# Filter spectra of a Hyena layer worked out in pieces between the expert passes

## What is computed

```
def hyena_filters(n, f_w1, f_b1, f_freq, f_w2, f_b2, f_w3):
    z = concatenate([t, cos(bands * w), -sin(bands * w)])      # positions alone
    h = sin(freq * (z @ f_w1 + f_b1))
    h = sin(freq * (h @ f_w2 + f_b2))
    h = (h @ f_w3).reshape(n, 2, C_ORDER, C_WIDTH)             # forward and backward filters
    return h * exp(-t * deltas)

def bidir_long_conv(u, h_fwd, h_bwd, bias):
    k = concatenate([h_fwd[:1] + h_bwd[:1], h_fwd[1:], 0, h_bwd[:0:-1]])
    uf = rfft(u, n=2 * n); kf = rfft(k)                        # kf: the spectrum of the filter
    return irfft(uf * kf)[:n] + u * bias
```

```
def expert_block(args):
    xb, e = args
    a = silu(xb @ w1[e]) * (xb @ w3[e])
    return a @ w2[e]
```

## Time and profile before

| | us |
|---|---|
| runs (3) | 3553.43, 3557.12, 3560.2; median 3557.12 |
| profiled execution, its own time | 3554.69 |
| its span in the profile | 3553.0 |
| TensorE busy | 3077.8 (87%) |
| VectorE busy | 1046.0 (29%) |
| ScalarE busy | 746.7 (21%) |
| DMA queue of SyncE (q1) | 416.81 MB, 33.2% of 16 engines' span |

### The profile page before, as it was taken

One profiled execution on the slowest core, in us unless ns is written; L12 is line 12 of the kernel. 1 busy time (PEld: TensorE's weight loads), 2 busy tenths in 40 slices (PEclk: granted clock), 3 DMA queues, 4 the chain that ended last, 5 costly groups with the idle time before them and its releaser, 6 DMA issues. The chain is left out here.

```text
span 3553.0 us, 34681 instructions
## 1 busy us (share of the span) xinstructions
PE 3077.8 (87%) x13906; PEld 1838.1 (52%) x13906; DVE 1046.0 (29%) x2162; ACT 746.7 (21%) x1627; POOL 164.0 (5%) x265
## 2 busy tenths in 40 slices
PE   6999974888887688999898999899948774888998
PEld 3448633444444655675455664465523343464674
DVE  3440622000000201254210472333025674200242
ACT  2111720000000202342200581100002210212341
POOL 0000001011111000000000120011100001000000
PEclk9999995899989899999999999999969887999999
DMA  6663441999999111200012100122233323011200
GB/s 229 232 232 131 174 153 44 380 377 384 386 386 337 60 53 32 76 1 24 1 36 72 72 2 1 45 84 97 77 108 155 129 77 124 0 42 55 76 1 24
DMA packets 244208, 441.15 MB, mean 124 GB/s; under 512 B 31420, under 2 KB 111820, under 8 KB 240725
## 3 DMA queue, kind: packets, MB, share of 16 engines
q1 hardware_dynamic: 234278, 416.81, 33.2%
q0 software_dynamic: 9776, 22.18, 1.8%
HBM read 408.73 MB, written 37.81 MB: 126 GB/s over the span
## 5 line engine op out<-in xcount | busy, mean ns | idle before, releaser
L347 PE MATMUL hyena_in_main<-hT,weight_slots 128*128 128x256 f32 (+1 forms) x1024 | 330.5, 486 | 1.4 <-PEq L988 1.4
L347 PEld LDWEIGHTS hyena_in_main<-hT,weight_slots 128*128 128x128 f32 x1024 | 194.6, 190 | 137.1 <-issue 124.0
L2006 PE MATMUL moe_ph<-expert_weights,moe_x_T 128*64 128x256 f32 x2048 | 235.8, 384 | 1.4 <-ACT moe_x_T L2159 1.4
L347 PE MATMUL swa_in_main<-hT,weight_slots 128*128 128x512 f32 (+1 forms) x576 | 189.3, 489 | 6.5 <-DMA weight_slots<-b_w_in 5.2
L2006 PEld LDWEIGHTS moe_ph<-expert_weights,moe_x_T 128*64 128x64 f32 x2048 | 144.6, 138 | 91.0 <-issue 24.7
L347 PE MATMUL mla_down_main<-hT,weight_slots 128*128 128x512 f32 (+1 forms) x448 | 168.6, 539 | 19.5 <-DMA weight_slots<-a_w_in 19.5
L1407 PE MATMUL qkv_main<-hT,weight_slots 128*128 128x512 f32 (+1 forms) x384 | 167.8, 580 | 0.9 <-PEq L988 0.9
L1198 PE MATMUL post_y<-expert_weights,hT 128*128 128x512 f32 x384 | 165.1, 592 | 0.0
L2023 PE MATMUL moe_py<-expert_weights,moe_act_T 128*64 128x512 f32 x512 | 161.4, 789 | 0.5 <-ACT moe_act_T L2166 0.5
L347 PEld LDWEIGHTS swa_in_main<-hT,weight_slots 128*128 128x128 f32 x576 | 110.0, 191 | 86.3 <-issue 73.7
L1996 PE MATMUL moe_px<-const_identity,moe_x 64*128 64x64 f32 x512 | 71.1, 294 | 90.1 <-DMA moe_x<-scr_tokens,moe_index 90.1
(11 more groups left out here) (357 smaller groups left out, 4117.4 us busy)
## 6 DMA issues: line engine op xcount, KB each, us to landing
expert_weights<-w SPq DMA_DIRECT2D x96, 2048.0 KB, 15.0
first_w_out<-w_mod SPq DMA_DIRECT2D x12, 2048.0 KB
expert_weights<-w_mod SPq DMA_DIRECT2D x12, 2048.0 KB, 8.0
weight_slots<-w_in SPq DMA_DIRECT2D x16, 1024.0 KB
weight_slots<-c_w_in SPq DMA_DIRECT2D x16, 1024.0 KB
weight_slots<-a_w_in SPq DMA_DIRECT2D x14, 1024.0 KB
scr_spectra<-expert_weights SPq DMA_DIRECT2D x12, 1024.0 KB, 3.8
expert_weights<-scr_spectra SPq DMA_DIRECT2D x12, 1024.0 KB, 5.3
```

What stands on the lines that cost most here:

```text
L347: mm = pe.matmul(main[u][0:unit.rows, 0:unit.cols], lhsT, rhs, start=(c == 0), stop=(c == r.kc - 1))
L2006: mm = pe.matmul(bank[half * T:(half + 1) * T, 0:HF], x_T[:, c, :], w[:, c, half * HF:(half + 1) * HF], start=(c == 0), stop=(c == KD - 1))
```

## The change

`filter_hidden` and `filter_spectra` are gone. Their work is in a class `FilterWork`, called from the streams of TensorE, ScalarE and VectorE in `experts_stage`. Each pass has three slots: slot 3b behind `turn_act`, 3b + 1 behind `turn_x`, 3b + 2 behind `down`. The two hidden products are in slots 2 and 5, with their six VectorE steps in the same slots and the Sin in slots 4 and 7; the sums of the filter weights are in slot 3. From slot 9 on 72 pieces are dealt out in order: 24 of filter rows (two products each) and 48 transform products (two 128x128 tiles each for x, one for the context). By the formula below they fall on slots 9 to 93, so into passes 3 to 31: 25 in slots 3b, 19 in 3b + 1, 28 in 3b + 2. Three PSUM banks are used in turn instead of eight; only the even products are copied by ScalarE, and VectorE forms sum and difference with the odd one straight from PSUM, in steps of 512 columns. The 12 stores of 1024 KB, three small loads and the load of the second half of the decays are issued by ScalarE, the stores two slots after their last product.

The other inputs (17 loads) are issued by SyncE in the route stage behind its own, which then waits for them. SyncE waits at the end of the expert stage for all spectra to be stored, before it issues `tiles` and the weight groups ahead. The eight transform tables of the convolution are loaded at the start of `hyena_in` (`beside`). `combine` takes its tiles from the arena of the expert weights, and the norm before the route takes its scratch from the weight slots.

```diff
@@ class FilterWork
+    SLOTS = 3
+    HID0, SIN0, HID1, SIN1, SUMS, FIRST = 2, 4, 5, 7, 3, 9
...
+        for j, (_, _, seg) in enumerate(self.jobs):
+            nb = SEGS[seg][2]
+            for c in range(2 * nb):
+                self.add(("rows", j, c), freed_by, ["rows", "rows"], cost, 1)
+            for k in range(nb):
+                for kind in range(KINDS):
+                    self.add(("kind", (j, k), kind), freed_by, ["odd" if kind % 2 else "even"], cost, nb)
+        self.banks = Banks(3, freed_by)
+        room, total, spent = self.SLOTS * (E - 1) - self.FIRST, sum(cost), 0
+        self.slot_of, taken = {}, set()
+        for piece, c in zip(self.pieces, cost):
+            slot = max(self.FIRST + spent * room // total, max(taken, default=0) + 1)
+            self.slot_of[piece] = slot
...
+    def on_tensor(self, pe, slot):
+        def free(q):
+            if q >= 3:
+                n = self.banks.upto(q - 3)
+                by = self.banks.freed_by[q - 3]
+                if by == "rows":
+                    pe.wait_ge(self.s_rows, n)
+                elif by == "even":
+                    pe.wait_ge(self.s_even, n)
+                else:
+                    pe.wait_ge(self.s_K, 2 * n)
+            return self.bank_of(q)
...
+            pe.wait_ge(self.s_rows, self.rows_upto(j))
+            pe.wait_ge(self.s_lag, j + 1)
+            b = free(q)
+            for c in range(nb):
+                row = kind % 2 * nb + c
+                mm = pe.matmul(b, table[seg][:, row, k * P:(k + 1) * P], src[:, row, :], start=(c == 0), stop=(c == nb - 1))
...
+    def on_scalar(self, act, scalar, slot):
...
+            act.wait_ge(self.s_K, 4 * (t + 1))
+            act.dma_start(self.spectra[SPECTRA.index((order, half, seg, k))], self.K[t % 2])\
+                .then_inc(self.s_stored[t % 2], 16)
...
+            act.wait_ge(self.s_mm, self.first_bank[piece] + 1)
+            if n >= 2:
+                act.wait_ge(self.s_K, 2 * (n - 1))
+            scalar.activation(self.parts[n % 2], self.bank_of(self.first_bank[piece]), ACT.Copy).then_inc(self.s_even, 1)
...
@@ def experts_stage
+                filters.finish(sp)
                 for tile, src in tiles:
                     sp.dma_start(tile, src).then_inc(s_tiles, 16)
@@ TensorE
                     if b:
                         turn_act(b - 1)
+                    filters.on_tensor(pe, n_slots * b)
                     pe.wait_ge(Stage.w3_in[b % 2], (b // 2 + 1) * 16)
                     pe.wait_ge(s_act, b)
                     up_product(pe, ph3, x_T[b % 2], experts.W3[b % 2]).then_inc(s_h3, 1)
                     if b + 1 < E:
                         turn_x(b + 1)
+                    filters.on_tensor(pe, n_slots * b + 1)
                     if b:
                         down(b - 1)
+                    filters.on_tensor(pe, n_slots * b + 2)
@@ VectorE
                 for b in range(E):
+                    filters.on_vector(dve, nc.vector, n_slots * b)
                     dve.wait_ge(s_silu, b + 1)
...
                     nc.vector.tensor_tensor(act_rows[:], ph3[:, 0:HF], act1[:], ALU.mult).then_inc(s_act, 1)
+                    filters.on_vector(dve, nc.vector, n_slots * b + 1)
                     if b:
                         copy_y(b - 1)
+                    filters.on_vector(dve, nc.vector, n_slots * b + 2)
@@ def route
+                for tile, src in beside:
+                    sp.dma_start(tile, src).then_inc(s_beside, 16)
+                sp.wait_ge(s_beside, 16 * len(beside))
@@ def hyena (was hyena_in and hyena_mix)
-    with nc.sbuf_tensor("filter_h2", [P, TOK], F32) as h2:
-        filter_hidden(nc, a, h2, tables)
-        filter_spectra(nc, a, h2, tables, spectra, g0, hT, left, consts)
-
+    hyena_in(nc, a, hT, scr, taps, consts,
+             [(tile, rows(a[f"{name}{2 * SEGS[seg][2] * P}"])) for (name, seg), tile in tables.items()])
```

More of the change, by code:

```diff
@@ L247, in load_down, with project @@
         sp.dma_start(self.W2[e % 2], self.w2[e]).then_inc(Stage.w2_in[e % 2], 16)
-def project(nc, name, ranges, consts, ahead=None, copies=()):
+def project(nc, name, ranges, consts, ahead=None, copies=(), beside=()):
     n_units = max(len(r.units) * (2 if r.apart else 1) for r in ranges)
@@ L322, in _ @@
                     load_ahead(sp, w, ahead)
+                if beside:
+                    sp.wait_ge(s_beside, 16 * len(beside))
             @block.tensor
@@ L1765, in route_constants, with route @@
     return c
-def route(nc, a, hT, gates, rest_experts, table, consts):
+def route(nc, a, hT, gates, rest_experts, table, consts, beside):
     R = E_GROUPS + E
@@ L1971, in _, with __init__, upto @@
                 pool.wait_ge(s_table, table0 + 16 * (2 * XT + 1))
+MAGIC = 1.5 * 2.0 ** 23
+TURN_HI = 6.28125
+TURN_LO = 2.0 * math.pi - TURN_HI
+SIN_END = 3.1415925
+HALF = D // 2
+SEGS = {"x": (0, 0, XT // 2), "ctx": (X, XT, CT // 2)}
+H_CHUNKS = XT + CT
+SPECTRA = [(order, half, seg, k) for order in range(2) for half in range(2) for seg in ("x", "ctx")
+           for k in range(SEGS[seg][2])]
+KINDS = 4
+class Banks:
+    def __init__(self, n, freed_by):
+        self.n, self.freed_by = n, freed_by
+    def upto(self, q):
+        return sum(1 for by in self.freed_by[:q + 1] if by == self.freed_by[q])
@@ L2467, in moe @@
         rest_experts, gates = sb("rest_experts", [P, REST + 1], I32), sb("gates", [P, 2, XT])
+        filters = FilterWork(nc, ctx, a, hT, slots, late)
         with ExitStack() as inner:
@@ L2472, in moe @@
             norm_and_turn(nc, "norm_ffn", [Normed(x, XT, D, hT, 0, lambda c: g[:, c:c + 1], row=row, dest=tokens)],
-                          consts)
-        route(nc, a, hT, gates, rest_experts, table, consts)
-        experts_stage(nc, experts, tokens, table, results, consts, tiles, following)
+                          consts, slots)
+        route(nc, a, hT, gates, rest_experts, table, consts, filters.loads())
+        experts_stage(nc, experts, tokens, table, results, consts, tiles, following, filters)
         rest_stage(nc, experts, rest_experts, tokens, table, results, consts)
-        combine_experts(nc, x, results, gates)
+        combine_experts(nc, experts, x, results, gates)
+        return filters.spectra
 A_WIDTH = A_HEADS * A_V
 B_WIDTH, B_KVW = B_HEADS * HD, B_KV * HD
[L2482 to L2485, removed]
 def second_constants():
@@ L3248, in hyena_mix, with second_block @@
     long_conv(nc, a, v, g0, tables, spectra, scr, a["c_w_out"][0], left, consts)
-def second_block(nc, a, x, hT, consts, out, modulation, experts, ctx, rope, ctx_out=None,
+def second_block(nc, a, x, hT, consts, out, modulation, experts, ctx, rope, slots, late, ctx_out=None,
                  layers=range(LAYERS)):
@@ L3271, in second_block @@
                  (taps[:], a["taps"])] + rope_loads
-        moe(nc, a, x, hT, consts, experts, tiles, first_range(layers[0]))
+        spectra = moe(nc, a, x, hT, consts, experts, tiles, first_range(layers[0]), slots, late)
         def room_of_layer():
@@ L3332, in build @@
         first_block(nc, a, x, hT, consts, modulation, experts, probs)
-        second_block(nc, a, x, hT, consts, out, modulation, experts, ctx_rows, rope)
+        second_block(nc, a, x, hT, consts, out, modulation, experts, ctx_rows, rope, flat, late[:])
 def kernel(**inputs):
```

415 lines of the change are left out of this document (194 added, 221 removed).

## The result

| | before | after |
|---|---|---|
| median of the runs, us | 3555.27 (4 runs) | 3431.0 (4 runs, 3424.46 to 3433.8) |
| span of the profiled execution, us | 3553.0 | 3429.5 |
| first load of `combine` | 1159.80 | 1186.21 |
| first load of `turn_tokens` | 2745.33 | 2620.43 |

The changed kernel takes 0.9646 of the time (95% interval 0.9633 to 0.966), 124 us less. The forecast was 3453, with 3424 to 3484 as its range.

A forecast was written before the change was run, and what follows sets the result against it. The prediction took the DMA engines to bound the expert passes, with TensorE and the gather loop close behind. 3554.7 - 150.8 + 37 + 3 + 8 = 3451.9 us, written as 3453 for the median; range 3424 to 3484.

The forecast's parts named there:

- The third layer: Third layer: two stages go, and the first load of `turn_tokens` takes the place of their first DMA, -150.8 us.
- Route: Route stage: 17 added loads, 5.1 MB, in a stretch with little traffic, 0 to 1 us; with no cover, 13.
- The DMA engines as the bound: Expert passes: added stores and decays load on full DMA engines make 18.2 us a pass, +37 us in all.
- rival (a): Expert passes absorb the added work, the clock may keep up; stage +12 us, 3427 us in all; chance 0.20.
- TensorE: Expert passes: with the pieces 17.9 us a pass at the present clock (+30 us), 16.2 at full clock (-19 us).
- The loop: Expert passes, copy through gather to down product: only 19 pieces lie in it, 0.4 us a pass, +12 us.
- The sine layers: Expert passes 0 and 1: two products, VectorE steps and filter weight sums, counted at half, +3 us (0 to 10).
- The end of the stage: End of the expert stage: SyncE waits for all spectra stores before issuing the next loads, +8 us (5 to 12).
- (b): Expert passes: each of 12 stores delays a gather by 3.5 us; stage +54 us, 3469 us in all; chance 0.16.
- (c): Expert passes: all pieces lie in series because TensorE is the real bound; +94 us, 3509 us; chance 0.07.
- (d): Expert passes: TensorE's waits for filter banks drop its clock, slower than before; at 0.70 +180 us, 3595 us; chance 0.03.
- (e): Third layer: the two stages do not really go, something else held 2594 to 2745; no change in time; chance 0.01.

The follow-up runs named there:

- the filler in the loop: The kernel before with two more products in each of passes 3 to 31, between the turning of x and the down product: 3647.8 us, ratio 1.0265.
- the filler: The kernel before with two more products in each of passes 3 to 31, before the second up product, outside the loop: 3547.61 us, ratio 0.9984.

## Why the prediction was right, and where it was off

**The third layer.** Forecast -150.8 us, measured -151.3. The first load of `turn_tokens` took the place of the first load of the hidden stage, and nothing new stood there.

**Route.** Forecast 0 to 1 us. The stage's stretch has 111 GB/s instead of 6 and the last of the 8 indirect DMAs is issued at 594.3 instead of 594.8. Right.

**The DMA engines as the bound.** The mechanism was right: the sign named for it, TensorE waiting for expert weights, is in the profile, and removing or doubling the stores moves the time nearly as their bytes would. The transfers alone, without a piece of work, cost 22 and 27 us of the same 37. So the size was off. Two of the other signs would have misled: the mean pass of 17.6 us and the clock of 0.99 are nearer to those of rival (a) (17.3 and 1.0) than to the 18.2 us of the forecast, and (a)'s 3427 us is nearer to the result than 3453. The loads' 21.8 us to landing also lie under the 25 to 30 that were named. Only the weight waits and the run without stores tell the two apart.

The term was 37 us. The growth up to the start of the last down product is 23.1 us, 1141.24 to 1164.38, where that product waits for its weights:

```profile
1163.43 0.33 ACTq L2188 DMA_DIRECT2D scr_spectra<-weight_slots  x1
1164.38 3.65 PE L2315 MATMUL moe_py<-expert_weights,moe_act_T 128*64 128x512 f32 x16 [0.99 <-DMA expert_weights<-w]
...
1167.39 0.37 SPq L2380 DMA_DIRECT2D ctx_rows_and_rope<-ctx  x1
...
1169.55 1.00 POOL L2329 DMA_INDIRECT scr_expert_rows<-moe_y,moe_index  x1 [3.97 <-DVE moe_y L2488]
...
1186.21 4.98 SPq L2746 DMA_DIRECT2D expert_weights<-scr_expert_rows  x8
```

The step that failed is "the DMA share of 1.04 in the row leaves nothing free". Two things were free. The rate rose from 383 to 388 GB/s, which over the 521 us in which the weights flow is 521 x 5 / 388 = 7 us. And the loads could run later before anybody waited. Near the end of the stage, among the loads issued from 1060 to 1120, the median time to landing was 17.6 us in the kernel before and is 23.5 in the changed one, another 6 us:

```profile
expert_weights<-w SPq DMA_DIRECT2D x10, 2048.0 KB, 17.6
...
expert_weights<-w SPq DMA_DIRECT2D x11, 2048.0 KB, 23.5
```

37 - 7 - 6 = 24, against 23.1 measured. That division is an estimate from the rows, and no run separates its parts. The prediction had this "time in hand" as a bound (23 us) and chose the other end; it let the time to landing grow to 30 us before TensorE waits, while the waits began at some 24. Its subtraction also gives 25 from 37 us, and 23 only from the 34.5 us of the 410 GB/s slice.

**TensorE.** Forecast 17.9 us a pass if the clock stayed, 16.2 if it rose; it rose, to 0.99. Rival (a) was right about the clock and wrong about the end: the gap closed and the clock came up, the pieces alone cost only 2.0 us, but then the bytes held the passes. The 90 us of idle time on which (a) and the reading of the kernel before rested were 66 of recurring gaps and 24 of the wait for the first gather. And at full clock, without stores, a pass was 16.68 us, not 16.2; where the 0.5 us lie is not shown. In the sum it was not needed which of the two clocks came, since the DMA term was the larger.

**The loop.** Its term, 0.4 us a pass, was mis-sized by half: it took 0.43 us for a call, which is one of its two recorded products. The 19 pieces in the loop are 11 of filter rows, 1.04 us each in the spectra stretch (24.9 us for 24), and 12 transform calls of 0.89 us (71.1 us for 80), so 22 us in 29 passes, 0.8 a pass. It did not reach the result, since the loop got 1.7 us a pass back from the clock, and moving the pieces out of it changes nothing.

**The sine layers.** Forecast +3 us, measured none. The load of W2 that the kernel before issues at 655.3 is issued at 653.5; the two products took 1.5 us each at the full clock, and `act_rows` of pass 1 was made 1.5 us later (632.66 against 631.15) without a later pass losing by it.

**The end of the stage.** Forecast +8 us. From the last scatter's issue to the mark it is 16.7 us instead of 13.4, +3.3; two of them come back with the tiles loaded early. The 8 us assumed that SyncE's chain would end the stage 8 us after a scatter that stayed where it was. But the last store could be issued ahead of the last down product, which itself waited for its weights, so the two chains ran side by side.

**Together**: -151.3 + 23.1 + 3.3 = -124.9 us at `turn_tokens`, against the forecast -102.8. The whole miss, 22 us, is the DMA term's 14, the end's 5 and the sine layers' 3; all three were too dear, none made up for another.

**The other rivals.** (b) fell, and in part for want of meetings: it let each of the 12 stores meet a gather, but only three gathers of the changed kernel ran wholly or mostly beside a store (issued at 788.28, 916.43 and 1040.67). They took 6.9, 6.5 and 7.4 us, within the 6.1 to 8.0 us of the others, where (b) had some 10 (6.7 + 3.5). (c), everything in series, fell: 2.0 us instead of 94. But the run with the filler in the loop shows that it was no idle fear: products between the turning and the down product, with the gap left open, cost nearly twice their length there. (d) fell: the clock rose. (e) fell: the third layer lost 151.3 us.

## What to carry to other kernels

Before work is moved beside a stream of loads, price its bytes and its products apart: here 94 us of products cost 2 us or so, and 14 MB of transfers alone cost 22 to 27, whichever queue issued them. When a stage has a closed loop with a short idle time in it, put the moved work outside the loop and into the gap; there it can pay for itself through TensorE's clock, as the filler did, and inside the loop it cost its length at the lower clock. Transfer engines that look full may still have a few per cent of rate and a few microseconds of lateness in hand: here the first four stores cost nothing, and all the time was lost behind them.

## What the runs showed of the hardware

- A gap of some 2 us before the turning in each pass of 16.9 us went with a granted clock of 0.90; closing it with 1.7 us of products gave 0.98, and 3.2 us of pieces a pass 0.99 to 1.00. Adding 50 us of products shortened the kernel by 6 us.
- A store of 1024 KB took 3.8 us to landing in the spectra stage and 7.5 to 8.6 us beside the weight loads. The gather took 3.0 to 3.2 us before these loads began, and then 6.2 to 7.8 us in the kernel before and 6.1 to 8.0 in the changed one.
- TensorE began to wait for expert weights when the loads took some 24 us from issue to landing (24.7 in the median of those issued from 820 to 880); in the kernel before, the highest median of such a stretch of 60 us was 18.8, and it never waited.
- When the weight loads run late, SyncE's issue of a load takes longer. Between 700 and 1120 most issues took 0.37 us in the kernel before, some up to 7; in the changed one most took 2 to 11 us (8.71 us in the pass above). SyncE had nothing else to do here; what such an issue would cost an engine that has other work was not measured.
- Between 700 and 1120 the rate was 383 to 389 GB/s in all twelve profiles with a DMA share of 1.04.
